# Decode attention inside prompt attention, linear attention ahead of both, key splits moved into the projection

## The reference, cut to what matters

```python
z = rms_norm(x, norm_w) @ w_in          # one projection, D = 1024; q, k, v, gate of attention,
                                        # q, k, v, gate and decay input of linear attention
# prompt attention, 4 heads, two score maps (m = 0, 1) of 64 channels, values 128 wide
s = q[m] @ k[m].T * scale + rel_bias(n) # causal, bias by distance
p = softmax(s[0]) - lam * softmax(s[1])
o = p @ v
# decode attention: the same with keys and values gathered from cache_k, cache_v by page_table
# linear attention: chunks of 128 with a decaying state S (prompt and 8 sequences)
y = x + concat(sub_norm(o) * silu(gate), norm(gla) * silu(gate_g)) @ w_out
```

## Time and profile before

| | PE | PEld | DVE | ACT | POOL |
|---|---|---|---|---|---|
| busy us | 1038.3 | 868.5 | 584.6 | 490.0 | 254.2 |
| share of the span | 82% | 69% | 46% | 39% | 20% |

### The profile page before, as it was taken

The page is one execution under the profiler, slowest core; times in us unless marked ns, Lnnn a source line. Parts: engine busy times, 40 slices in busy tenths (PEclk is TensorE's granted clock), DMA queues, the critical chain, the costliest instruction groups (busy, mean ns, idle before and its releaser), DMA issues. The chain is left out here.

```text
span 1259.8 us, 27242 instructions
## 1 busy us (share of the span) xinstructions
PE 1038.3 (82%) x9055; PEld 868.5 (69%) x9055; DVE 584.6 (46%) x1430; ACT 490.0 (39%) x1383; POOL 254.2 (20%) x399
## 2 busy tenths in 40 slices
PE   4999999999999487879878887467788836777998
PEld 4999999997999466556655654155667625664886
DVE  4755522302222134443443443277878458868221
ACT  5644314613424223333333432156767345533110
POOL 0000000000000222343434341222211159800000
PEclk9999999999999799999999998558999967787999
DMA  5312332212111699999999999530000052102221
GB/s 169 93 38 95 106 122 80 82 34 76 53 49 49 215 386 338 385 387 387 387 387 387 387 387 169 148 111 9 17 10 13 1 175 74 51 26 69 97 89 60
DMA packets 106820, 195.21 MB, mean 155 GB/s; under 512 B 14406, under 2 KB 48652, under 8 KB 106732
## 3 DMA queue, kind: packets, MB, share of 16 engines
q1 hardware_dynamic: 85716, 126.03, 30.8%
q0 software_dynamic: 20480, 67.13, 14.3%
q10 hardware_dynamic: 536, 0.89, 0.2%
HBM read 174.41 MB, written 19.60 MB: 154 GB/s over the span
## 5 line engine op out<-in xcount | busy, mean ns | idle before, releaser
L843 POOL DMA_DIRECT2D vraw<-in_cache_v x256 | 137.6, 537 | 667.7 <-issue 663.8
L512 PE MATMUL pz<-wh,xTh 128*128 128x256 f32 (+1 forms) x864 | 248.7, 288 | 0.0
L512 PE MATMUL pz<-wh,xTl 128*128 128x256 f32 (+1 forms) x864 | 244.3, 283 | 0.0
L512 PE MATMUL pz<-wl,xTh 128*128 128x256 f32 (+1 forms) x864 | 244.2, 283 | 0.0
L925 PE MATMUL pk<-ident,kraw 128*128 128x128 f32 x1024 | 136.7, 291 | 57.0 <-DMA kraw<-in_cache_k 54.0
L925 PEld LDWEIGHTS pk<-ident,kraw 128*128 128x128 f32 x1024 | 121.8, 150 | 70.9 <-DMA kraw<-in_cache_k 62.0
L863 DVE COPY kt<-pk 128x512 f32<-128x512 f32 x128 | 82.9, 687 | 183.1 <-PE pk L925 182.1
L512 PEld LDWEIGHTS pz<-wh,xTh 128*128 128x128 f32 (+1 forms) x864 | 160.6, 186 | 1.6 <-issue 1.2
L512 PEld LDWEIGHTS pz<-wh,xTl 128*128 128x128 f32 (+1 forms) x864 | 160.7, 186 | 0.0
L512 PEld LDWEIGHTS pz<-wl,xTh 128*128 128x128 f32 (+1 forms) x864 | 160.5, 186 | 0.0
L643 DVE SCALAR_TENSOR_TENSOR wl<-wraw,nw,wh 128x256 fp32r<-128x256 f32 x112 | 52.3, 482 | 117.1 <-ACT wh L358 116.2
(11 more groups left out here) (241 smaller groups left out, 1857.5 us busy)
## 6 DMA issues: line engine op xcount, KB each, us to landing
kraw<-in_cache_k SPq DMA_DIRECT2D x256, 256.0 KB, 9.6
vraw<-in_cache_v POOLq DMA_DIRECT2D x256, 256.0 KB, 5.7
wraw<-in_w_in SPq DMA_DIRECT2D x14, 1024.0 KB, 5.6
out<-nat SPq DMA_DIRECT2D x32, 128.0 KB, 1.8
xb<-in_x_prompt SPq DMA_DIRECT2D x7, 512.0 KB, 3.6
xr<-in_x_prompt SPq DMA_DIRECT2D x7, 512.0 KB, 3.5
out<-xr SPq DMA_DIRECT2D x7, 512.0 KB, 2.6
val_d<-nat SPq DMA_DIRECT2D x16, 128.0 KB, 1.8
```

The lines of the kernel that those rows point to most:

```text
L512: ins = pe.matmul(z_at(u)[0:r, 0:CB], a[:, k, P * i:P * i + r], b[:, c % 2, k, :], start=(n == 0), stop=(n == 3 * KT - 1))
L843: pool.dma_start(vraw[:, g % VR, n, :], cache_v.rearrange("a n p h d -> (a n) p (h d)")[bass.ds(page, 1)] .rearrange("o p c -> (o p) c")). ...
```

## The change

The blocks become A, G, M, O, where M holds decode and prompt attention together. SBUF is laid out by hand (class `Area`, offsets given) in place of the allocator.

In A, the keys are no longer kept as kT but written as their two parts `ks`: ACT makes the high parts (two copies of 64 partitions a key tile), DVE the rests (`key_lo`), and PE's turn of a key tile waits for the rest of the one two before. w_in comes in half blocks with three slots of half a block. The 16 columns of the decay input are loaded once by a DMA of their own and scaled by one DVE operation. Other buffers are reused for x and for squares.

In G, seven small bias inputs are loaded ahead of the other loads, PE makes the biases first, DVE adds them after the second tile's factors, and SP issues the four skewed writes ahead of the values and gates of tile 2. The page table is loaded here. w_out is not.

In M, the key ring has 6 pages (16 before), the value ring 8 (16), `kt` one buffer (two), turned keys two banks by page (four by head), decode scores, turned probabilities and gathered sums share one bank `px`, prompt turns have one bank (three). ACT copies pages 0 and 2 of a group, DVE pages 1 and 3. POOL makes all four query rests of a tile. Score widths are exact. w_out is loaded at the end of SP's list. Decode is unrolled and cut into 7 steps a group, 9 groups a row (the last one for the new tokens) and 9 rows, 569 steps in all. Each of the 32 units takes a share of them, 5 + i of 272 for tile i, in four segments; every engine has its own list of what it does in a step, and steps with nothing in them for that engine are empty.

```diff
+            SUBS = 7
+            NSUB = (NB + 1) * RG * SUBS + 2
+            share = [5 + units[u][0] for u in range(LAST0)]
+            def upto(u, seg):
+                if u >= LAST0:
+                    return NSUB
+                done = sum(share[:u]) + share[u] * (seg + 1) / 4
+                return NSUB if (u, seg) == (LAST0 - 1, 3) else int(NSUB * done / sum(share))
...
+            @block.tensor
...
+                        for g in range(G):
+                            for n in range(GRP):
+                                if kb is not None:
+                                    turn_keys(kb, g, n)
+                                yield
+                            if b is not None:
+                                turn_probs(b, g)
+                            yield
+                            if b is not None and g >= 1:
+                                values_c(b, g - 1)
+                            yield
+                            if kb is not None:
+                                scores_c(kb, b, g)
+                            yield
...
+                for u in range(NU + 1):
+                    before = batches(u - 1) if u >= 1 else []
+                    if u < NU:
+                        scores(u, 0)
+                    go(u, 0)
+                    if before:
+                        turn(before[0])
+                    go(u, 1)
+                    if len(before) > 1:
+                        turn(before[1])
+                    if before:
+                        values(before[0])
+                    go(u, 2)
+                    if len(before) > 2:
+                        turn(before[2])
+                    for b in before[1:]:
+                        values(b)
+                    if u < NU:
+                        scores(u, 1)
+                    if u >= 1 and mix_after(u - 1) is not None:
+                        turn_mix(mix_after(u - 1))
+                    go(u, 3)
...
+            @block.scalar
...
+                        for g in range(G):
+                            if kb is not None and g >= 1:
+                                scores_out(kb, g - 1)
+                            if b is not None:
+                                expo_c(b, g)
+                            yield
+                            if kb is not None:
+                                copy_keys(kb, g, 0)
+                            yield
+                            yield
+                            if kb is not None:
+                                copy_keys(kb, g, 2)
...
+                    go(u, 0)
+                    if before:
+                        turned(before[0])
+                    if u < NU:
+                        expo(u, 0)
+                    go(u, 1)
+                    if len(before) > 1:
+                        turned(before[1])
+                    go(u, 2)
+                    if len(before) > 2:
+                        turned(before[2])
+                    if u < NU:
+                        expo(u, 1)
...
+            @block.vector
...
+                for u in range(NU + 1):
+                    if u >= 1:
+                        combine(u - 1)
+                    if u < NU:
+                        maxima(u, 0)
+                    for seg in range(3):
+                        go(u, seg)
+                    if u < NU:
+                        maxima(u, 1)
...
+                    go(u, 3)
...
+                for i in range(2, TILES):
...
+                    load_v(i)
-                        for k in range(KT):
-                            sp.dma_start(wo_raw[k], w_out[0, k * P:(k + 1) * P, :]).then_inc(wo_in, 16)
...
-            wraw = sb(st, "wraw", [P, 2, KT, CB])
+            wraw = m.take("wraw", [P, 3, KT // 2, CB])
...
+                            pe.wait_ge(klo_done, count(("k",), s - 2))
```

More of the change, by code:

```diff
@@ new lines, in hymba_kernel @@
+        ident = low.take("ident", [P, P])
+        lam = low.take("lam", [P, 8])
+        nlam = lam[:, 7:8]
+        pages = low.take("pages", [1, NB * NPAGES], I32)
+        kn = low.take("kn", [P, H, NS])
+        dlast = low.take("dlast", [P, PAGE])
+        dnew = low.take("dnew", [32, NB * NS])
+        qT = low.take("qT", [P, H, NTOK])
+        ks = low.take("ks", [P, 2, H, L], F32R)
+        mixT = low.take("mixT", [P, 2 * H, NTOK])
+        FREE = low.at
+        MIXD = FREE - 4 * 2 * H * NTOK
@@ L181, in hymba_kernel @@
             LOGS = GA + 1
+            BLOCKS = [c for c in range(len(KINDS)) if c != GA]
+            wslot = lambda c: BLOCKS.index(c) % 2
             CH = [(0, 384), (384, 384), (768, NTOK - 768)]
@@ L348, in x_hi, with w_hi @@
                            .then_inc(xhi_done, 1)
[L350 to L358, removed]
+                def w_hi(c, at=range(KT)):
+                    if at[0] == 0 and c >= 2:
+                        act.wait_ge(z_done, BLOCK_END[BLOCKS[BLOCKS.index(c) - 2]])
+                    for k in at:
+                        x = half_of(c, k)
+                        act.wait_ge(w_loaded[x % 3], 16 * (x // 3 + 1))
+                        act.activation(wh[:, wslot(c), k, :], raw(c, k), ACT.Copy, scale=nw[:, k:k + 1])\
                            .then_inc(whi_done, 1)
@@ L710, in log_decay, with key_lo @@
                     dve.wait_ge(lg_done, i + 1)
+                def key_lo(s):
+                    if kind(s) != "k":
+                        return
+                    c, i = natural[s]
+                    two = slice(2 * (c % 2), 2 * (c % 2) + 2)
+                    n = P if i < TILES - 1 else TAIL
+                    of = pn[:, s % 2, 0:2 * P].rearrange("p (h t) -> p h t", h=2)
+                    dve.wait_ge(nt_out, s + 1)
+                    for m in range(2):
+                        ins = dve.tensor_tensor(ks[own[1 - m], m, two, P * i:P * i + n], of[own[m], :, 0:n],
+                                                ks[own[m], m, two, P * i:P * i + n].bitcast(F32), ALU.subtract)
+                    ins.then_inc(klo_done, 1)
                 for s in range(NN + 1):
@@ L716, in _ @@
                             finish(s - 1)
[L717 removed]
+                            for b in (GA - 1, LOGS):
                                 w_lo(b)
@@ L832, in _ @@
-            @block.gpsimd
-            def _(pool):
-                def load_values(b, peeled):
-                    for g in range(G):
-                        if not (peeled and g < VR):
-                            pool.wait_ge(pv_done, b * (G + 1) + (g - VR + 1 if g >= VR else g - VR))
-                        if peeled and g == VR - 2:
-                            pool.wait_ge(band_out, 1)
-                        for n in range(GRP):
-                            page = pool.value_load(pages[0:1, bass.ds(b * NPAGES + GRP * g + n, 1)],
-                                                   min_val=0, max_val=POOL - 1)
-                            pool.dma_start(vraw[:, g % VR, n, :],
-                                           cache_v.rearrange("a n p h d -> (a n) p (h d)")[bass.ds(page, 1)]
-                                           .rearrange("o p c -> (o p) c")).then_inc(v_in[g % VR], 16)
-                load_values(0, True)
-                with pool.Fori(1, NB) as b:
-                    load_values(b, False)
```

1823 lines of the change are left out of this document (928 added, 895 removed).

## The result

The changed kernel takes 1306.5 us (median of 4 runs, 1301.2 to 1310.9) against 1265.3 before: ratio 1.031, 95% interval 1.026 to 1.036, slower. The profiled execution has a span of 1306.2 us.

The account below looks back on a forecast made before the run. Transfer-bound decode C and prompt attention B, bound by chains between engines (599.9 us together), would overlap in M at 585; 1263.7 - 15 (M) + 4 (G) + 2 (A) = 1255 us, own range 1232 to 1278, with rivals 1178 to 1308.

Parts of the forecast that it names:

- For the clock I add 8: In M: 8 us for a low granted clock at its start, as B's first 29 us were granted 0.50.
- R2: Rival, all of PE in M: recurring small waits lower the granted clock; at 0.88 M 631, total 1301; chance 0.21.
- Steps 1 to 7: PE's program through M, start to tail unit: 583 us, less 12 for waits falling together: 571; weight loads add 6.
- step 2: In M, row 0 of decode turns keys and makes scores, no probabilities yet: 8 groups x 4.2 = 33.5 us.
- step 3: In M, decode rows 1 to 7: 4.55 us a group instead of 3.87, through waits for copies; 297 us.
- step 6: In M, ACT's per-tile output scaling and squares, query copies and mix copy in one piece: 27 us show on PE.
- Step 5: In M, decode's key copies queue behind prompt maxima and exponential: 3.0 us a unit at 8 blocks, 45.5 in all.
- G, forecast +4: G: +4 us (-3 to +13): later first loads 3, bias results 1.4, tile 2 behind skewed writes 0, 10 at most.
- A and O: A: key splits lie beside PE's products, gate weights' load +2 us (-2 to +8); O: same products, 0.
- POOL nothing: In M, POOL's four query splits a tile, 6 us in one piece ahead of value loads, cost nothing; 11 otherwise.
- R1: Rival in M: the streams hide each other, 45 + 27 us of stalls vanish; M 512, total 1182; chance 0.27.
- R3: Rival: late key and value pages in M, or G's tile 2 late: +10 to +25 us, total 1270; chance 0.11.

Follow-up runs that it names:

- sized filling: Changed kernel plus 130 idle matmuls in PE's waits (14 at each of seven tile ends, 8 at four row ends): 1296.4 us, 1.024.
- late places: Changed kernel with the prompt's instructions on ACT and DVE placed later among the decode steps: 1279.0 us, 1.009.
- Decode first: Changed kernel with all 569 decode steps in the first unit's first segment, no interleaving: 1479.0 us, 1.171.
- two queues: Kernel with late places, spread skewed writes and spread query rests, with SP issuing the odd value pages of every row: 1257.1 us, 0.994.
- splitting a long piece: ACT's output scaling and squares done head by head: on the changed kernel 1317.8 us (1.040), on late places with spread loads 1273.4 us (1.005).

## Why the prediction was wrong, step by step

It forecast 1255 us, 9 faster; it is 41 slower than the runs of before beside it.

- **Failed: the term "For the clock I add 8".** I priced the clock as a start effect, from B's first 29 us at 0.50, and put it at nothing for the rest of M. It costs 56.3 us in M, and the start, up to 579, is only about 2 of them. The 48 us between 56.3 and 8 are those by which M, 633.7, lies above 585. By the same count C and B had lost 37 already, which I never added up. The sized filling shows that most of this time is real and that it follows from PE's waits.
- **R2 was the outcome, with its number and not quite its mechanism.** It gave M 631 and 1301 at a mean clock of 0.88; measured 633.7, 1306.5 and 0.87. But the small waits, recurring each microsecond, did not pull the clock down: it stayed at 1.00 through the 36 us from 579.5 with PE busy 78%. The long waits did, at tile ends, query copies and row ends, as at tile 4 with most of 800 to 808 at the lower level. The Trainium skill (TensorE: Matmul & The Clock Gate, A second HAM failure mode: psum-queue depth-cycling) describes a clock that swings between its levels because of short, frequent idle times between groups of matmuls; in this trace it swings too, but behind waits of about 5 us and not in the stretch with waits under 1 us.
- **Steps 1 to 7 held in their sum**: work and idle 577.5, forecast 577. That it is so close is partly luck. R2 put PE's work at some 400 us, which leaves 177 for waits; measured were 416 and 161. Two slips nearly cancel: step 2's own terms with step 3's waits of 0.67 give 3.4 us a group and not 4.2, 6 us less; step 6 took 1.26 us for four query copies, where the earlier trace rows has 629 ns for each and the trace after 2.53 for four, 7 us more. Step 5's reading, key copies queued behind maxima and exponential, was right; the late places took 27 us off. Step 3's 4.55 us a group was not read alone.
- **Where the gain went.** C's waits for transfers and B's gaps were to hide each other. Decode first at 1479 shows that the two do hide much of each other in this block, by 172 us. But the room for both was paid with single buffers, and PE idles 161 in M, against 145 in C and B. That these buffers' waits are what gives the gain back is argued from the waits for key copies; no run has larger buffers.
- **G, forecast +4, measured +10.5.** The 3 for later first loads was right (3.8). "0 taken, 10 at most" for tile 2 behind the skewed writes was the wrong end; spreading them gave 7.3 in that block.
- **A and O** (+2, 0) were right. "POOL nothing" was about its query rests: spreading them left the waits for values as they were (27.4 and 30.4), so no run shows a cost of that piece behind the start. What it left out was that POOL issues all the values alone: with two queues 30.4 us of waits became 3.9.
- **R1** did not occur; its "each under 75%" is 75.8% for PE over C and B. **R3** occurred in G's part; in M, keys cost 2 us, and of the 15 for values 11 came in the last row, not at the first tiles. Its 366 GB/s is 384 with 2.1 MB a group.

Open: what the smaller rings alone cost, and why M of one kernel varies by 7 us between profiled executions (633.7, and 626.4 with only G changed). A's key splits were not run alone.

## What to carry to other kernels

A wait costs more than its length where the engine's clock falls after it: price a stretch by the granted clock that rows with the same waits show, not by the best row. When two streams share in-order engines, put the second stream's long operations on each engine as late as its consumer allows, so that short copies which free a buffer go first; that order was worth 27 us here, while splitting a long piece made the kernel slower both times. The Trainium skill (Perfetto Trace Analysis, Identifying Performance Opportunities) says that interleaving regimes with different bounds may help; it did, by 172 us against the same block in sequence, and still lost to two blocks with larger buffers.

## What was not expected of the hardware

130 matmuls whose results nobody reads, 31 us of PE, did not make the kernel slower but 10 us faster by the medians: they kept the granted clock at 1.00 at tile 4's end, where it had been 0.53 and 0.62 for 8 us, and took 20 us off what the clock cost in M. And four writes of 192 KB from one SBUF partition each, laid out in rows of 1.5 KB, took 82% of the DMA engines' time at 26 GB/s, and loads of 256 KB issued behind them landed after 9 to 11 us in place of 3.
